# One stream for prompt and sample attention: page chunk scores and logits first in their step, and a half's sum of values in three parts

## The reference

```python
o = g[:, :, :, 0] * o_cmp + g[:, :, :, 1] * o_sel + g[:, :, :, 2] * o_win
```

## Time and profile before

| | us |
|---|---|
| median of 3 runs | 2594.09 (2593.25 to 2598.07) |
| profiled execution | 2593.48 |
| its span | 2591.5 |
| PE busy | 2311.3 (89%) |
| DVE busy | 1090.8 (42%) |
| ACT busy | 695.3 (27%) |
| POOL busy | 416.3 (16%) |
| mean granted PE clock | 0.942 of 2.4 GHz |

### The profile page before, as it was taken

How to read it: one execution, slowest core, us unless ns; L and a number is a source line. 1 busy time by engine, 2 the same in 40 slices (tenths; PEclk the granted TensorE clock), 3 DMA queues, 4 the chain that set the end, 5 groups by cost and what they waited for, 6 DMA issues and landing times. The chain is left out here.

```text
span 2591.5 us, 41142 instructions
## 1 busy us (share of the span) xinstructions
PE 2311.3 (89%) x15977; PEld 2092.9 (81%) x15977; DVE 1090.8 (42%) x2461; ACT 695.3 (27%) x1391; POOL 416.3 (16%) x374
## 2 busy tenths in 40 slices
PE   8999675876888887999899969899999999999995
PEld 7799664774555556999798956699999999999995
DVE  2212355125566573122217203427755555553335
ACT  3210153103555563011135002435211111121122
POOL 0000011320322211212111100011212212222220
PEclk9999887788999998999899989999999999999997
DMA  3211203877433423111131043512111111111212
GB/s 135 96 48 49 15 1 104 282 255 273 165 133 104 134 84 104 49 49 42 62 107 33 17 146 131 199 49 96 46 49 49 41 49 49 38 40 49 108 41 75
DMA packets 114348, 233.22 MB, mean 90 GB/s; under 512 B 23442, under 2 KB 76339, under 8 KB 110723
## 3 DMA queue, kind: packets, MB, share of 16 engines
q1 hardware_dynamic: 85034, 177.94, 20.9%
q0 software_dynamic: 10368, 28.33, 3.3%
q10 hardware_dynamic: 18754, 24.35, 2.7%
HBM read 207.28 MB, written 27.47 MB: 91 GB/s over the span
## 5 line engine op out<-in xcount | busy, mean ns | idle before, releaser
L88 PE MATMUL psum<-x_half_high,ff_half 128*128 128x352 f32 x3240 | 792.2, 324 | 13.9 <-DVE h_again_low L69 9.0
L88 PEld LDWEIGHTS psum<-x_half_high,ff_half 128*128 128x128 f32 x3240 | 568.6, 189 | 15.2 <-DVE ff_half L69 9.2
L88 PE MATMUL psum<-h_again_low,ff_half 128*128 128x352 f32 x1176 | 379.0, 322 | 0.0
L69 POOL TENSOR_TENSOR ff_half<-ring,ff_half 128x1024 fp32r<-128x1024 f32 (+2 forms) x85 | 177.2, 2086 | 760.9 <-ACT ff_half L3048 760.9
L88 PEld LDWEIGHTS psum<-h_again_low,ff_half 128*128 128x128 f32 x1176 | 222.8, 189 | 0.0
L88 PE MATMUL psum<-merged_high,oq_half 128*128 128x352 f32 x768 | 190.0, 328 | 13.0 <-DVE oq_half L69 12.8
L3048 ACT ACTIVATE ff_half<-ring 128x1024 fp32r<-128x1024 f32 (+2 forms) x88 | 78.0, 888 | 433.5 <-PE psum L88 407.3
L88 PE MATMUL psum<-mid_low,ff_half 128*128 128x352 f32 x516 | 167.0, 324 | 0.0
L88 PEld LDWEIGHTS psum<-merged_high,oq_half 128*128 128x128 f32 x768 | 136.4, 192 | 13.5 <-DVE oq_half L69 13.1
L1706 PE MATMUL psum<-consts,na_p 128*128 128x128 f32 x528 | 86.5, 303 | 50.5 <-DVE na_p L1987 41.2
L1706 PEld LDWEIGHTS psum<-consts,na_p 128*128 128x128 f32 x528 | 62.0, 152 | 83.5 <-DVE na_p L1987 58.9
(11 more groups left out here) (551 smaller groups left out, 4232.6 us busy)
## 6 DMA issues: line engine op xcount, KB each, us to landing
na_kv<-in_pool SPq DMA_DIRECT2D x128, 128.0 KB, 3.5
na_kv<-in_pool POOLq DMA_DIRECT2D x128, 128.0 KB, 4.0
sab_kv<-in_pool SPq DMA_DIRECT2D x96, 128.0 KB, 4.4
mg_w<-in_w_merge SPq DMA_DIRECT2D x16, 768.0 KB, 4.4
sab_kv<-in_pool POOLq DMA_DIRECT2D x88, 128.0 KB, 4.7
ring<-in_f_wu SPq DMA_DIRECT2D x22, 512.0 KB, 3.7
ring<-in_f_wg SPq DMA_DIRECT2D x22, 512.0 KB, 3.7
sab_kv<-in_pool ACTq DMA_DIRECT2D x72, 128.0 KB, 4.6
```

What stands on the lines that cost most here:

```text
L69: return engine.tensor_tensor(low, x, high.bitcast(F32), ALU.subtract)
L88: ins = nc.tensor.matmul(out, w[a], x[b], start=first and n == 0, stop=last and n == 2)
```

## The change

Two edits. A PAGES item's scores and logits take the same place in their step as all others: first on PE, ahead of turn and values, and ahead of factors on DVE. And `combine` becomes three functions, called at the end of three following steps of DVE, the first in the step in which the half's last chunk is stored.

```diff
             for n in range(-3, U):
-                paged = n + 3 < U and items[n + 3][0] == PAGES
-                if n + 3 < U and not paged:
+                if n + 3 < U:
                     scores(n + 3)
                 if 0 <= n + 1 < U:
                     turn(n + 1)
                 if n >= 0:
                     values(n)
-                if paged:
-                    scores(n + 3)
...
-            def combine(s):
+            def sum_factors(s):
                 ve.wait_ge(S["weight_ready"], s + 1)
...
                 ch.link(nc.vector.tensor_tensor(fac[:, s, WINK:WINK + 1], ssums[:, s, WINK:WINK + 1], gr[:, s, 2:3], ALU.mult))
+
+            def weighted_values(s):
                 ch.link(nc.vector.tensor_tensor(pv[:, :, :], pv[:, :, :], fac[:, s, 0:CHUNKS].unsqueeze(2).to_broadcast([P, CHUNKS, P]), ALU.mult))
+
+            def add_values(s):
                 if s:
                     ve.wait_ge(S["between_ready"], 2)
                 ch.link(nc.vector.tensor_reduce(acc[:, :], pv[:, :, :].rearrange("p k d -> p d k"), AX.X, ALU.add))
...
                     nc.vector.sem_inc(S["between_kept"], 1)
-                    if t == LASTC:
-                        combine(p)
                     return
...
+            SUM_PARTS = (sum_factors, weighted_values, add_values)
+            last_chunk = [at[PAGES, s, LASTC] for s in range(2)]
...
             for n in range(-3, U + 1):
                 if n >= 1:
                     store(n - 1)
-                paged = n + 3 < U and items[n + 3][0] == PAGES
-                if n + 3 < U and not paged:
+                if n + 3 < U:
                     logits(n + 3)
                 if 0 <= n + 2 < U:
                     factors(n + 2)
-                if paged:
-                    logits(n + 3)
+                for s in range(2):
+                    if 0 <= n - last_chunk[s] - 1 < len(SUM_PARTS):
+                        SUM_PARTS[n - last_chunk[s] - 1](s)
```

## The result

| | before | after |
|---|---|---|
| median of the runs | 2594.89 us (2593.25 to 2598.07, 4 runs) | 2571.74 us (2567.40 to 2572.84, 4 runs) |
| ratio, 95% interval | | 0.9906 (0.9889 to 0.9923) |
| profiled execution | 2593.48 us | 2567.40 us |
| its span | 2591.5 us | 2565.6 us |
| PE busy | 2311.3 us | 2302.4 us |

The kernel is 23.2 us faster by the medians (0.8 to 1.1%), where 29.7 was forecast; the time lies inside the range. Most code lines of after have numbers one to four lower: `turn` is L1705, page scores L1649, the other scores L1666, the scaling L1983, page logits L1841.

A forecast was written before the change was run, and what follows sets the result against it. TensorE was taken as the bound, except where it waits for VectorE's scaling. Terms -15.0 - 4 + 1.7 - 4 - 2.8 - 5.6 = -29.7 us on 2593.5 us, forecast 2564.4 us against the median; range 2554 to 2580.

The forecast's parts named there:

- Page scores first, and the bank: TensorE's page steps: page scores fill the wait ahead of the turn, 15.0 us; their PSUM bank is free sooner, 4 us.
- Page logits ahead of the scaling: VectorE's page steps: the SLIDE scaling now stands behind page logits, hidden by VectorE's idle time, 0 us.
- Loads late: Page scores ask for their chunk earlier; two of four tight chunks look late, +1.7 us, bounds 0 and 6.
- Rival A: Chunk loads become the wait, landing 2 to 3 us later: 12 us back, 2576 us; chance 0.11.
- The clock: TensorE runs less at 1.2 GHz behind shortened waits in seven page rounds: 4 us gained, bounds 0 and 9.
- First half's sum: Sum split in three on VectorE, scaling first, TensorE goes on sooner: 2.8 us gained, bounds 0 and 7.9.
- Second half's sum: Split sum removes TensorE's 4.27 us wait and the slow turn behind it: 5.6 us gained, bounds 4.3 and 6.2.
- The shift stays: Behind the sparse attention stage nothing has a time of its own, so the stage's gain carries through.
- range's own ends: The forecast's own extremes: 2556 us with all clock and bank time back and no late load; 2576 at worst.
- Rival D: Slower: TensorE stands for loads at the step's head, delaying the next loads; 2606 us at 16.5 us landings; chance 0.04.
- Rival C: Early page scores are held by the bank or TensorE's order; only the split sum gains, 2586 us; chance 0.04.
- Rival B: VectorE comes late with the SLIDE scaling behind page logits: 12 us back, 2576 us; chance 0.04.

The follow-up runs named there:

- e12: The changed kernel, unchanged, run once more beside later experiments; 2565.27 us, ratio 0.9882 to the kernel before.
- e3: Changed kernel with page logits put back behind factors on VectorE, page scores still first on TensorE; 2568.94 us, ratio 0.9891.
- e4: Kernel before, plus four matmuls at the head of each page step whose result is overwritten and unused; 2588.01 us, ratio 0.9961.
- e8: Changed kernel with the first half's CLOSE item moved two query tiles later; 2567.72 us, ratio 0.9883.
- e10: Changed kernel with the first half's product and chunk sum on POOL, last two adds on VectorE, CLOSE item two tiles later; 2564.20 us, ratio 0.9877.
- e1: Changed kernel with combine put back as one piece, new order kept; 2575.01 us, ratio 0.9909.
- e2: Changed kernel with the old order put back in both loops, the sum still in three parts; 2589.10 us, ratio 0.9962.
- e5: Changed kernel with half of each chunk's loads left out, so samples attend to partly old data; 2561.97 us, ratio 0.9860.
- e6: Changed kernel with POOL issuing twelve of a chunk's sixteen loads and SP four; 2572.57 us, ratio 0.9890.
- e9: Changed kernel with SP loading all keys, released once scores two chunks before are done, and POOL all values, in half-size loads; 2588.22 us, ratio 0.9966.

## Why the prediction was right, and where its sizes were off

The stream gave 29.2 us in the profile, and the prediction's sum was 29.7; the medians gave 23.2, and 31.8 in e12. The mechanism and the largest terms were right. That the sum is so close is luck: the clock gave some 3 us more than forecast, page scores and bank 1 and the second half 0.6, the loads took 2.6 more (without their half clock) and the first half's sum gave 2.6 less.

- **Page scores first, and the bank: 15 + 4, right together.** No run has them apart. Together they are what remains: 29.2 of the stream, less 6.2 (second half), 0.2 (first half) and 7 (clock), plus 4.3 for the loads (5.8 less 1.5 that is half clock and counted there), is 20.1. The rows bear it out: from one page item's `values` to the next, in the rounds with neither half clock, nor a late load, nor a wait of 0.54, after gains 0.9 to 1.4 us. The old waits of 1.6 to 2.45 us became page scores and 0.9 us or less. The bank's share shows in the SEL scores, 1.99 us for 2.15.
- **Page logits ahead of the scaling: 0, right.** Shown by e3.
- **Loads late: +1.7, mis-sized.** It measured 2.4 in e12 and 5.8 in after (1.5 of it half clock), just under the upper bound of 6. The arrival was right (8.8 us behind the release, measured 8.84), and it was the four tight chunks that came late. Two things failed. The sum let the scores start with the last packet, and they started 0.7 to 1.0 us behind it in all four: in the known round the last packet ended 8.8 us behind the release, much as forecast (9.0), and the scores started at 9.8. And the landing varied: the scores started 11.7 us behind the release at 777.79, and in e12 that same chunk took 775.73 - 765.15 = 10.6 us. A tie needs the spread of the landing, not its usual value. Rival A's mechanism is thus in the result, at up to half its 12 us; it took no more because the 0.9 us cushion stood in each turn.
- **The clock: -4, mis-sized.** e4 puts the seven stretches at 8.5 us; less the one new (1.5), 7. Taking "less than half", since the waits don't vanish, was the step that failed.
- **First half's sum: -2.8, mis-sized; measured 0.2 (0.7 in e12)**, near its lower bound. The waits came as worked out, 1.51 for 1.4 and 2.03 for 2. But the half clock was taken for gone (until 814 before), and behind 1.5 + 2.0 us of idle time it came again, from 802 to 812. The lead of after over before is 7.46 us just ahead of the sum and 7.62 behind it. VectorE's busy time in those short steps (1.93 of 2.00 us and 2.33 of 2.40) and e8, where the wait only moved, speak for VectorE as the bound there; e10, which was to prove it, couldn't.
- **Second half's sum: -5.6, right**, measured 6.2: the wait 4.27, the turn 3.83 to 2.55, the `values` behind it 1.93 to 1.31.
- **The shift stays: not quite.** 2.2 and 2.6 us were lost ahead of the stream and 1.5 gained behind it, where nothing was changed, and the medians' 23.2 has such parts in it. The prediction had no term for these: the kernel before alone had medians from 2594.9 to 2600.1 us, so some 3 us to either side belong to any forecast of this kernel.
- **A slip in the range's own ends:** 2564.4 with all clock (5 more) and bank time (0.4 more) back and no late load (1.7 less) is 2557.3, not 2556. The range doesn't hang on it.
- **Rival D, slower**: landings of 15.4 us didn't come; the longest found was 11.7. The feared rule stands in "SBUF — State Buffer", section "🔬 SBUF: two separate sides", of the Trainium skill, that VectorE in a two-port mode keeps GpSimd from writing descriptors. No run shows it at that size. In the known round no scaling lies beside POOL's issues; where two do, eight issues took 4.69 to 4.95 us, against 4.69 to 4.70 elsewhere. One such place (timelines of POOL, then of DVE):

```profile
748.79 4.76 POOL L1530 DMA_DIRECT2D na_kv<-in_pool  x8 [8.20 <-PE psum L1732]
...
749.23 1.27 DVE L1983 TENSOR_SCALAR na_p<-na_p,na_rs,branch_gates 128x768 f32<-128x768 f32 x2
751.77 1.14 DVE L1983 TENSOR_SCALAR na_p<-na_p,na_rs,branch_gates 128x640 f32<-128x640 f32 x2
```

- **Rival C** (only part 2 counts) is ruled out by e1 and e2: the order alone gives 24.3 of the 30.8 us. **Rival B** is ruled out by e3.

## What to carry to other kernels

When an engine waits in a fixed place of its program for another, look for work of its own that is ready by then and move it there: it gains its own time, and by shortening the wait it can also keep TensorE's clock up, which here was worth another third (7 us beside 20). Then ask what the moved work itself waits for, take the slowest of its transfers, not the usual one, and count the time from the last packet to the first matmul. Splitting a block of work in parts only helps where the engine has slack in the steps to which the parts go; where it is the bound, the wait moves on.

## What the runs showed that had not been expected

- The granted clock stood at 1.2 GHz behind seven of the waits of before and behind the one of 2.82 us in after, but not behind the one of 2.25 us there, though behind one of 2.04 in e8; behind those of 0.9 us in e4 and e5 it never did. In e2, which has the page waits of before, it did so behind six, one of them another: which waits are hit changes from execution to execution. Four matmuls that compute nothing of use made a kernel 0.25 to 0.53% faster.
- POOL's tensor operations held up VectorE's scalings, 2.67 us instead of 0.74 (e10); POOL's DMA issues beside the same kind of scaling did not (1.14 us for two of 128x640 at 751.77, as without them at 679.32 before).
- The time from POOL's last issue to the page scores is not fixed: 4.4 us behind eight issues, 2.2 behind twelve (e6). For the same chunk in the same program they started 11.7 and 10.6 us behind its release (after, e12). In all four late chunks of after the last packets were those of POOL's queue.
- Reading eight page numbers from the table costs a queue 4.4 us (e9), as much as issuing the eight loads (4.68).
